# Hybrid layer with a hierarchical MoE on one core: expert rows stored even features first, both transposes of a unit in one stretch, gathers ahead of scatters

## The reference, cut to what matters

```python
v  = modulate(layer_norm(x), shift, scale)          # rows that the experts read
le = (vf @ w_re + b_re)                             # router, from the same rows v
...
hb = silu(xb @ w_gate[e]) * (xb @ w_up[e])          # xb: rows of v gathered for expert e
y  = hb @ w_down[e]
ys = ypad[dest] * gate                              # scattered back, summed per token
```

## Time and profile before

| | |
|---|---|
| median of 3 runs | 1596.18 us (1595.07 to 1599.83) |
| the profiled execution | 1595.59 us, span of its records 1593.6 us |
| PE busy | 1383.2 us, 87% of the span |
| DVE / ACT / POOL busy | 60% / 35% / 19% |
| DMA | 365.84 MB, 230 GB/s on average |
| mean granted clock | 0.946 |

### The profile page before, as it was taken

How to read it: one execution, slowest core, us unless ns; L and a number is a source line. 1 busy time by engine, 2 the same in 40 slices (tenths; PEclk the granted TensorE clock), 3 DMA queues, 4 the chain that set the end, 5 groups by cost and what they waited for, 6 DMA issues and landing times.

```text
span 1593.6 us, 37050 instructions
## 1 busy us (share of the span) xinstructions
PE 1383.2 (87%) x13489; PEld 1025.5 (64%) x13489; DVE 955.0 (60%) x1696; ACT 559.7 (35%) x869; POOL 302.1 (19%) x316
## 2 busy tenths in 40 slices
PE   4799999979999997899996399999989999977771
PEld 3688989978888885685885355555545555543330
DVE  6755645778888998876766742423352423443459
ACT  4322223425666566422231042414342323342210
POOL 4000002210000001000000133433443433423300
PEclk8999999999999998999998699999999999997886
DMA  9666307543344336532237698966998949989752
GB/s 285 205 235 242 110 27 226 161 138 121 108 135 144 113 121 240 202 98 85 73 112 296 237 399 338 367 269 234 400 407 344 378 177 377 407 350 407 295 216 102
DMA packets 169583, 365.84 MB, mean 230 GB/s; under 512 B 16040, under 2 KB 94944, under 8 KB 166312
## 3 DMA queue, kind: packets, MB, share of 16 engines
q1 hardware_dynamic: 150616, 308.72, 53.0%
q0 software_dynamic: 18320, 54.08, 9.7%
q10 hardware_dynamic: 576, 2.10, 0.4%
HBM read 324.06 MB, written 45.63 MB: 232 GB/s over the span
## 4 chain that ended last, share of the span: by engine, by line
PE 39%; DVE 7%; issue 5%; DMA 3%; ACT 3%; DVEq 2%; SPq 1%; ACTq 0%; POOLq 0%
PE PS L2147 16%; PE PS L2022 10%; PE PS L2165 6%; DMA ring<-in_w_down_dram 3%; ACT ring L1965 2%; PE PS L2156 2%; PE PS L2201 1%; PE PS L2135 1%; DVE big L2217 1%; PE PS L2053 1%; PE PS L2088 1%; DVEq L2482 1%; PE PS L2045 1%; DVE ring L2567 1%; DVE st L2559 0%
## 5 line engine op out<-in xcount | busy, mean ns | idle before, releaser
L939 PE MATMUL PS<-big 128*128 128x344 f32 x2592 | 423.7, 323 | 1.7 <-DVE big L1192 1.7
L939 PEld LDWEIGHTS PS<-big 128*128 128x128 f32 x2592 | 412.7, 190 | 10.4 <-issue 6.7
L2147 PE MATMUL PS<-ring,arena 128*32 128x256 f32 x5248 | 324.9, 394 | 15.8 <-DVE arena L2463 13.0
L2147 PEld LDWEIGHTS PS<-ring,arena 128*32 128x32 f32 x5248 | 183.2, 113 | 133.4 <-issue 47.1
L1965 ACT ACTIVATE ring<-ring 128x1024 f32 x124 | 121.3, 1046 | 137.0 <-SPq L1694 81.1
L1806 POOL DMA_INDIRECT arena<-v_d,icur x84 | 99.0, 1179 | 330.7 <-DVE icur L2475 241.4
L2165 PE MATMUL PS<-ring,arena 128*32 128x256 f32 x2624 | 158.6, 382 | 1.0 <-DVE arena L2471 1.0
L2492 DVE COPY ring<-ring 128x1024 f32 x124 | 78.4, 691 | 96.6 <-PE PS L2147 45.7
L1814 POOL DMA_INDIRECT f_d<-arena,scur x82 | 123.4, 1504 | 60.0 <-issue 36.4
L2463 DVE COPY arena<-PS 128x256 f32<-128x256 f32 x82 | 34.6, 422 | 129.2 <-PE PS L2135 129.2
L2165 PEld LDWEIGHTS PS<-ring,arena 128*32 128x32 f32 x2624 | 76.9, 109 | 53.4 <-DVE arena L2471 1.3
(11 more groups left out here) (434 smaller groups left out, 1868.1 us busy)
## 6 DMA issues: line engine op xcount, KB each, us to landing
ring<-in_w_gate_dram SPq DMA_DIRECT2D x32, 2048.0 KB, 10.5
ring<-in_w_up_dram SPq DMA_DIRECT2D x32, 2048.0 KB, 15.6
ring<-in_w_down_dram SPq DMA_DIRECT2D x32, 2048.0 KB, 8.9
arena<-in_w_ada_dram SPq DMA_DIRECT2D x16, 1024.0 KB, 5.4
arena<-in_w_in_dram SPq DMA_DIRECT2D x20, 512.0 KB, 6.1
upper<-in_w_ada_dram SPq DMA_DIRECT2D x8, 1024.0 KB, 11.4
upper<-in_w_in_dram SPq DMA_DIRECT2D x16, 512.0 KB, 3.8
arena<-acs_d SPq DMA_DIRECT2D x8, 1024.0 KB, 4.6
```

Of the source, the lines that this page charges most:

```text
L939: mm = pe.matmul(PS[:, 3 * b + a, 0:CU], wss[b][:, i, k, :], us[:, j, k, a * CU:(a + 1) * CU], start=(k == 0 and (i, j) == PARTS[0]), stop ...
L2147: mm = pe.matmul(PS[32 * g:32 * g + 32, 3, 0:FH], xT[:, c, CAP * q:CAP * q + CAP], wcur[:, w:w + FH], start=(q == 0 and c == 0), stop=(q = ...
```

## The change

- `V` is written with the 512 even features first and the odd ones behind (`apart`), reading its inputs with a step of two (`paired`). For the sample tile a copy does this. `wr` is loaded to match, in four DMAs in place of two. `x_turn` now reads contiguous columns, and `gate_up` picks its blocks of `xT` to match the weights, which lie as before.
- In PE's body x_turn(u+2) moves from behind gate_up(u+1) to in front of it, right behind h_turn(u).
- In DVE's body gather_rows(u+4) moves to the front, and waits for x_turn(u+2) itself.
- POOL does gather(u+4), scatter(u-1).

```diff
+        def paired(x):
+            return x.rearrange("p (m c) -> p c m", c=2)
+        def apart(x):
+            return x.rearrange("p (c m) -> p c m", c=2)
...
-                    sp.dma_start(dst, src.rearrange("(k p) n -> p k n", p=P)).then_inc(wr_loaded, 16)
+                    for c in range(2):
+                        sp.dma_start(dst[:, 4 * c:4 * c + 4, :], src.rearrange("(q p c) n -> c p q n", p=P, c=2)[c])\
+                            .then_inc(wr_loaded, 16)
...
                 with gp.Fori(1, pairs) as j:
                     for b in range(2):
                         gather(j * 2 + (b + 4), b)
-                        scatter(j * 2 + b, b)
+                        scatter(j * 2 + (b + -1), 1 - b)
...
-                        mm = pe.transpose(PS[:, 0, P * c:P * c + P], xg[b][:, c::2], ident[:, :])
+                        mm = pe.transpose(PS[:, 0, P * c:P * c + P], xg[b][:, P * c:P * c + P], ident[:, :])
...
-                                mm = pe.matmul(PS[32 * g:32 * g + 32, 3, 0:FH], xT[:, c, CAP * q:CAP * q + CAP],
+                                mm = pe.matmul(PS[32 * g:32 * g + 32, 3, 0:FH], xT[:, q % 2, CAP * (2 * c + q // 2):CAP * (2 * c + q // 2) + CAP],
...
                 with pe.Fori(1, pairs) as j:
                     for b in range(2):
                         h_turn(j * 2 + b)
+                        x_turn(j * 2 + (b + 2), j + 1, b)
                         gate_up(j * 2 + (b + 1))
-                        x_turn(j * 2 + (b + 2), j + 1, b)
                         down(j * 2 + b)
...
-                    row(ve.scalar_tensor_tensor(out=V[0:r, :], in0=x[0:r, :], scalar=mv[0:r, 0:1],
-                                                in1=(V if q == QD else sc2)[0:r, :], op0=ALU.subtract, op1=ALU.mult))
...
+                        row(ve.scalar_tensor_tensor(out=apart(V), in0=paired(x), scalar=mv[:, 0:1], in1=paired(sc2),
+                                                    op0=ALU.subtract, op1=ALU.mult))
...
+                    if q == QD:
+                        row(ve.scalar_tensor_tensor(out=O[0:r, :], in0=V[0:r, :], scalar=rstd[0:r, :], in1=O[0:r, :],
+                                                    op0=ALU.mult, op1=ALU.add))
+                        ve.tensor_copy(apart(V[0:r, :]), paired(O[0:r, :])).then_inc(v_ready, 1)
+                    else:
+                        ve.scalar_tensor_tensor(out=apart(V), in0=apart(V), scalar=rstd[:, :], in1=paired(sh2),
+                                                op0=ALU.mult, op1=ALU.add).then_inc(v_ready, 1)
...
                 def gather_rows(u, b):
+                    ve.wait_ge(eT_mm, u + -1)
                     ve.tensor_copy(icur[b][:, :], idxT[:, bass.ds(u, 1)]).then_inc(icur_ready, 1)
...
                     for b in range(2):
+                        gather_rows(j * 2 + (b + 4), b)
                         h_out(j * 2 + b)
                         up_copy(j * 2 + (b + 2), j * 2 + (b + 1))
                         x_out(j * 2 + (b + 2))
-                        gather_rows(j * 2 + (b + 4), b)
                         scatter_rows(j * 2 + b, j, b)
                         down_copy(j * 2 + (b + 1))
```

More of the change, by code:

```diff
@@ L1821, in _ @@
                 pairs = gp.value_load(ctl[0:1, CTL_N:CTL_N + 1], min_val=NE // 2 - 1, max_val=(NE + NOV) // 2 - 1)
-                for u in range(2):
-                    gather(u + 4, u)
-                    scatter(u, u)
+                gather(4, 0)
+                gather(5, 1)
+                scatter(0, 0)
                 with gp.Fori(1, pairs) as j:
@@ L1827, in _ @@
                         gather(j * 2 + (b + 4), b)
-                        scatter(j * 2 + b, b)
-                for b in range(2):
-                    scatter(pairs * 2 + b, b)
+                        scatter(j * 2 + (b + -1), 1 - b)
+                for u in range(-1, 2):
+                    scatter(pairs * 2 + u, u % 2)
             @block.scalar
@@ L2101, in _ @@
                     if q == 2:
-                        pe.wait_ge(wr_loaded, 64)
+                        pe.wait_ge(wr_loaded, 96)
                     if q == QD:
@@ L2176, in _ @@
                     h_turn(u)
+                    x_turn(u + 2, 1, u)
                     gate_up(u + 1)
-                    x_turn(u + 2, 1, u)
                     down(u)
@@ L2285, in norms @@
                         ve.wait_ge(vt_mm, q)
-                    row(ve.scalar_tensor_tensor(out=V[0:r, :], in0=x[0:r, :], scalar=mv[0:r, 0:1],
-                                                in1=(V if q == QD else sc2)[0:r, :], op0=ALU.subtract, op1=ALU.mult))
+                    if q == QD:
+                        row(ve.scalar_tensor_tensor(out=V[0:r, :], in0=x[0:r, :], scalar=mv[0:r, 0:1], in1=V[0:r, :],
+                                                    op0=ALU.subtract, op1=ALU.mult))
+                    else:
+                        row(ve.scalar_tensor_tensor(out=apart(V), in0=paired(x), scalar=mv[:, 0:1], in1=paired(sc2),
+                                                    op0=ALU.subtract, op1=ALU.mult))
                     ve.wait_ge(lns_ready, 2 * q + 2)
                     row(ve.reciprocal(rstd[0:r, :], rstd[0:r, :]))
-                    ve.scalar_tensor_tensor(out=V[0:r, :], in0=V[0:r, :], scalar=rstd[0:r, :],
-                                            in1=(O if q == QD else sh2)[0:r, :], op0=ALU.mult, op1=ALU.add)\
-                        .then_inc(v_ready, 1)
+                    if q == QD:
+                        row(ve.scalar_tensor_tensor(out=O[0:r, :], in0=V[0:r, :], scalar=rstd[0:r, :], in1=O[0:r, :],
+                                                    op0=ALU.mult, op1=ALU.add))
+                        ve.tensor_copy(apart(V[0:r, :]), paired(O[0:r, :])).then_inc(v_ready, 1)
+                    else:
+                        ve.scalar_tensor_tensor(out=apart(V), in0=apart(V), scalar=rstd[:, :], in1=paired(sh2),
+                                                op0=ALU.mult, op1=ALU.add).then_inc(v_ready, 1)
                 ve.sem_inc(yl_ready, 1)
@@ L2520, in _ @@
                 for u in range(2):
+                    gather_rows(u + 4, u)
                     h_out(u)
@@ L2523, in _ @@
                     x_out(u + 2)
-                    gather_rows(u + 4, u)
                     scatter_rows(u, 0, u)
```

## The result

The changed kernel took **1612.14 us** (median of 4 runs, 1610.51 to 1614.88) beside 1595.77 for the kernel before (4 runs, 1595.07 to 1599.83): ratio 1.0107, interval 1.0094 to 1.0121. Three later sets on other occasions gave 1.0086, 1.0105 and 1.0081. The forecast was 1582.

What follows compares the result with a forecast made beforehand. PE bounds plain expert units, ACT's ring gate-copy units, and weight transfers the two DMA-bound stretches. Gains 12.5 + 2.4 less 1.3 gave 13.6 us: 1595.6 - 13.6 = 1582.0, range 1572 to 1592.

Steps and rivals of the forecast that it cites:

- POOL, "Nothing in the sum": Expert units: gather u+4 right after x_turn u+2 and scatter landing 1 to 3 us later cost nothing in the sum.
- Gate-copy units, "nothing": Expert units copying new gate weights, 31 at 6.8 to 7.3 us: no gain; about 1 us of cover left.
- One stretch for both turns: Plain expert units: one load-width switch fewer and cheaper x_turn loads gain 0.29 us each, 43 x 0.29 = 12.5 us.
- The rule on 16-byte lines: Strided reads keep full bandwidth, so x_turn's loads would get no faster and the gain would be 0.14 a unit.
- Late x_out: Four units following DVE's down and up copies: x_turn and one switch leave the late gate_up's stretch, gaining 2.4 us.
- icur ahead of h_out: DVE's copy queued before h_out delays down in units with a down copy: 19 x 0.07 = 1.3 us lost.
- Storage of V: Norms before the expert units: storing even and odd features apart costs 0, ends 0 and +1.2 us.
- Rival 3: A late gather holds PE in front of gate_up; at 1 us over, time 1602; chance 0.10.
- the 12.5 us of the forecast: Gain over plain expert units outside DMA-bound stretches and late-x_out cases, 43 x 0.29.

Runs made afterwards that it cites:

- after_again: The changed kernel, run again unchanged on a chip of the first kind: 1611.1 us, 1.0086 of the kernel before.
- gated_again: The changed kernel with scatter u-1 also waiting for the end of gate_up u+1, repeated on the first kind of chip: 1588.1 us, 0.9932 of the kernel before.
- before_xfirst: The kernel before with x_turn moved ahead of gate_up on PE alone: 1592.1 us, 0.9973 of the kernel before.
- both_old: The changed kernel with gather_rows (icur) back behind x_out and POOL's old order: 1593.2 us, 0.9988 of the kernel before.
- gated: The changed kernel with scatter u-1 also waiting for the end of gate_up u+1: 1588.2 us, 0.9948 of the kernel before.
- gated_q3: The changed kernel with scatter u-1 waiting for the third quarter of gate_up u+1, second kind of chip: 1578.8 us, 0.9946 of the kernel before.
- before_gated: The kernel before with scatter u behind the second quarter of gate_up u+2, second kind of chip: 1586.2 us, 0.9995 of the kernel before.
- before_gated_again: The kernel before with scatter u behind the second quarter of gate_up u+2, repeated on the first kind: 1589.5 us, 0.9944.

## Why the prediction was wrong

- **POOL, "Nothing in the sum": this step failed.** I asked when the gathered rows land and when the scattered ones do. Both were in time but for the first unit, below. What I did not ask is what issuing does to others while it goes on. Before, gather and scatter stood 1.6 to 2.0 us apart in 39 of the 82 units and 1.5 or less in 27; I moved the scatter right behind the gather in nearly all, and both into narrow work. Priced by after_again and gated_again, on one chip: 1611.1 - 1588.1 = 23 us. Such pauses, 0.6 us on average, were in the trace of before already: one of 0.60 us in gate_up of the very unit of the earlier trace rows, whose scatter started 1.50 us behind its gather (timeline of before). I had read that unit for ACT's ring only.

```profile
1102.08 1.03 POOL L1806 DMA_INDIRECT arena<-v_d,icur  x1 [1.99 <-DVE icur L2475]
...
1103.58 1.03 POOL L1814 DMA_INDIRECT f_d<-arena,scur  x1 [0.47 <-issue]
...
1104.92 1.10 PEld L2147 LDWEIGHTS PS<-ring,arena 128*32 128x32 f32 x24 [0.60 <-issue]
```

- **Gate-copy units, "nothing": failed for the same reason.** Their median went from 7.5 to 8.0 us, and not because x_turn ate the cover: copies waited for PE's late signals. Forecast for the 32 intervals with copies: a small gain; measured +14.7 us.
- **One stretch for both turns, 0.29 us a unit: the size nearly held, the reason half.** Undisturbed units take 5.90, a gain of 0.36, and the second stop of the loads in a unit is gone, as forecast. But I had put 0.17 of it on the shorter loads, and they are worth 0.02. The loads did get as short as forecast (groups of PE's loads, before_xfirst with strided input and both_old with contiguous):

```profile
L2135 PEld LDWEIGHTS PS<-ident,arena 128*128 128x128 f32 x163 | 26.2, 203 | 17.9 <-DVE arena L2463 11.7 <-issue 5.1 <-DMA arena<-v_d,icur 0.9
```

```profile
L2143 PEld LDWEIGHTS PS<-ident,arena 128*128 128x128 f32 x164 | 19.8, 145 | 22.0 <-DVE arena L2479 12.5 <-issue 7.7 <-DMA arena<-v_d,icur 1.4
```

  203 against 145 ns, yet the units take 5.92 and 5.90 us, and the kernels 1592.1 and 1593.2. From h_turn's first load to gate_up's first it is 0.60 us with the long loads and 0.59 with the short ones; all but 0.02 of the gain is the place. The rule on 16-byte lines of the Trainium skill (SBUF — State Buffer, "Door 1: The DMA port swizzle"), which I had weighed, would have given no shorter loads: on the loads it is contradicted, on the time it would have been nearly right for the storage.
- **Late x_out, 2.4 us gained: it lost 2.3.** The four units took 36.1 us before and 38.5 after. My sum let x_turn leave the stretch behind the late gate_up. It only moved in front of it: x_turn waits for the same late x_out to free its PSUM, and gate_up queues behind it (timeline of the changed kernel):

```profile
1341.75 0.20 PEld L2143 LDWEIGHTS PS<-ident,arena 128*128 128x128 f32 x2 [1.95 <-DVE arena L2479]
```

  So the two units whose clock stayed as it was gained nothing (8.48 to 8.54 us, 9.90 to 9.93). In the other two the granted clock fell once gate_up started, which it had not before (busy time by stretch, after and then before; the column before the last two is the clock):

```profile
1029.20:1034.00 4.80, 4.80 (x61) 2.59 (x64) 1.98 (x6) 1.71 (x2) 2.34 (x2) 0.64 1.02 403
```

```profile
1024.20:1028.30 4.10, 3.79 (x62) 2.57 (x64) 1.42 (x4) 1.44 (x2) 2.40 (x2) 1.00 1.03 379
```

- **The first unit** went from 6.26 to 8.90 us: its x_turn, now ahead of gate_up, waits 1.33 us for gathered rows, where it had not waited before. The rest of the 2.6 us I have not traced.
- **icur ahead of h_out, -1.3 us**: of the right order. In gated, 10 of the 18 units with only a down copy take 5.90; in the other 8 down starts 4.2 to 4.6 us after h_turn and not at 3.9, and they take 3.3 us more together. How much of that is icur, and how much a down copy that starts late, was not separated. **Storage of V, 0**: right, its two operations take 1.28 us each, as before.
- **Rival 3** named the right engine and the wrong wait. Its mechanism, PE held by late rows, shows in the changed kernel in the first unit alone; in both_old it shows in nine waits, 5.2 us together.
- **The gain that was left.** With most pairs gone, gated is 8.4 us faster than the kernel before on the first kind of chip, gated_q3 9.1 on the other, not 13.6. On the other kind the 49 intervals without gate or up copies take 298.5 us in gated_q3 and 311.0 in before_gated: the 12.5 us of the forecast. But the 32 with copies take 276.0 and 273.6. Where weights set the pace a faster unit only waits longer: ACT's wait for SP is 90.4 us in gated_q3 and 85.8 in before_gated.

```profile
ACT ring L1975 <- SPq L1702: 90.4, 7, 33.9
```

And of the 8.4 us on the first kind, before_gated_again shows 7.1 to be the kernel before's own pauses: there the rest of the change adds 1.3 us, within the intervals. The plain units gain there too (303.4 us in gated_again, 311.1 in before_gated_again), and the units with copies lose it again (284.8 and 275.6). That PE's late signals behind the moved scatter cost them this fits the traces, but no run isolates it.

## What to carry to other kernels

When a DMA that an engine issues in software is moved, price its issue as an event for every other engine, not only its landing: look in the old trace for places where two such issues already stood close together, and compare the unit's length there with its neighbours'. A pause marked "issue" on an engine with nothing to wait for is worth laying beside the timeline of all engines before the order is changed. And measure on more than one chip: moving the kernel before's scatter gained 0.6% on one kind here and nothing on the other.

## What the runs showed that I had not expected

- On the first kind of chip two indirect DMAs of POOL started 1.3 to 1.5 us apart paused PE's weight loads for more than 0.3 us, and up to 0.7, in 357 of 469 cases; from 1.6 us on in none of 145. On the other kind in none of 14. What differs between the chips the runs do not show, nor by what path POOL's issuing reaches PE. (The Trainium skill, SBUF — State Buffer, "SBUF: two separate sides", has engines contend for the memory only at the port that POOL and DVE share; PE is none of the two, so by that rule the pause is not a contention of engine ports.)
- On the first kind a signal of PE arrived 1.3 to 1.8 us behind the start of a scatter if it was due sooner; behind a gather about 0.15 us late; on the other kind it arrived on time.
- The kernel before itself takes 1595.0 to 1596.9 us on chips 1, 3 and 4 and 1587.5 to 1587.9 on chips 5 and 6. Chips 3 and 4 were each measured twice and came out alike.
